# Ten expert loads ahead instead of six, whole experts for two of the three matrices, and further rounds before the last two quads

## The reference, cut to what matters

```python
for l in range(2):
    mod = silu(c) @ mod_w[l] + mod_b[l]        # 1024 x 6144: shift, scale, gate, twice
    h = rms_norm(x, norm1_g[l]) * (1 + scale1) + shift1
    x = x + gate1 * attention(h)               # w_in 1024 x 3072 (+8), w_out 1024 x 1024
    h = rms_norm(x, norm2_g[l]) * (1 + scale2) + shift2
    # router: one of 4 groups, then 2 of its 8 experts for each token
    # every expert: w1, w3: 1024 x 512, w2: 512 x 1024
    y = sum over experts of (silu(h @ w1[e]) * (h @ w3[e]) * gate[:, e]) @ w2[e]
    x = x + gate2 * y
```

## Time and profile before

| | |
|---|---|
| runs | 1378.91, 1379.0, 1375.66 us; median 1378.91 |
| the profiled execution | 1371.47 us, span 1369.7 us |
| data moved | 489.78 MB, 358 GB/s over the span |
| TensorE | busy 72% of the span, mean granted clock 0.868 |
| VectorE, ScalarE, GpSimd | busy 19%, 16%, 2% |
| experts of layer 0 and 1 | about 222 to 695 us and 893 to 1364 us |

### The profile page before, as it was taken

How to read it: one execution, slowest core, us unless ns; L and a number is a source line. 1 busy time by engine, 2 the same in 40 slices (tenths; PEclk the granted TensorE clock), 3 DMA queues, 4 the chain that set the end, 5 groups by cost and what they waited for, 6 DMA issues and landing times.

```text
span 1369.7 us, 13973 instructions
## 1 busy us (share of the span) xinstructions
PE 989.0 (72%) x5668; PEld 443.5 (32%) x5668; DVE 262.8 (19%) x573; ACT 213.9 (16%) x431; POOL 30.4 (2%) x89
## 2 busy tenths in 40 slices
PE   4999898667565766766679999967476675757665
PEld 1445555222121222222146665532121231212121
DVE  0545534101000010100020366410000010000101
ACT  2223314001000000100010353410000010000000
POOL 3000000000000000000000022000000000000000
PEclk9999999788887888888789999999887888878787
DMA  9973716999999999999999336569999999999995
GB/s 355 392 224 123 307 62 278 423 422 422 423 421 422 422 423 422 421 422 423 422 405 376 136 117 253 235 277 422 423 422 423 422 422 422 422 422 422 422 422 216
DMA packets 90826, 489.78 MB, mean 358 GB/s; under 512 B 18208, under 2 KB 18336, under 8 KB 37544
## 3 DMA queue, kind: packets, MB, share of 16 engines
q1 hardware_dynamic: 87776, 487.95, 87.4%
q10 hardware_dynamic: 3016, 1.37, 0.4%
HBM read 488.25 MB, written 1.05 MB: 357 GB/s over the span
## 4 chain that ended last, share of the span: by engine, by line
DMA 53%; PE 39%; DVE 4%; issue 1%; ACT 1%; SPq 1%; DVEq 0%
DMA ring<-in_moe_w_dram 52%; PE bank L546 8%; PE bank L788 7%; PE bank L813 7%; PE bank L586 4%; PE bank L699 4%; PE bank L511 2%; DMA ring<-in_mod_w_dram 1%; PE bank L638 1%; SPq L335 1%; PE bank L540 1%; PE bank L654 1%; PE bank L749 1%; PE bank L823 1%; DVE tmp L1404 0%
## 5 line engine op out<-in xcount | busy, mean ns | idle before, releaser
L788 PE MATMUL bank<-ring,region 128*32 128x512 f32 x2048 | 303.9, 748 | 189.2 <-DMA ring<-in_moe_w_dram 187.5
L813 PE MATMUL bank<-ring,region 128*32 128x512 f32 x1024 | 168.5, 818 | 122.9 <-DMA ring<-in_moe_w_dram 122.9
L788 PEld LDWEIGHTS bank<-ring,region 128*32 128x32 f32 x2048 | 83.6, 133 | 396.1 <-issue 394.4
L813 PEld LDWEIGHTS bank<-ring,region 128*32 128x32 f32 x1024 | 46.0, 143 | 232.7 <-issue 232.7
L546 PE MATMUL bank<-ring,hT 128*128 128x512 f32 x256 | 115.4, 602 | 2.7 <-ACT hT L953 2.7
L1542 DVE TENSOR_TENSOR region<-region,bank 128x512 f32<-128x512 f32 x16 | 11.0, 688 | 497.6 <-PE bank L788 497.6
L953 ACT ACTIVATE region<-bank,shift,scale 128x128 f32<-128x128 f32 x64 | 24.1, 457 | 353.2 <-PE bank L772 353.2
L1549 DVE TENSOR_TENSOR region<-bank,region 128x512 f32<-128x512 f32 x32 | 20.6, 686 | 281.1 <-PE bank L813 281.1
L823 PE MATMUL bank<-region 128*128 128x512 f32 x128 | 59.2, 605 | 13.4 <-DVE region L1549 13.4
L546 PEld LDWEIGHTS bank<-ring,hT 128*128 128x128 f32 x256 | 47.9, 193 | 59.4 <-issue 56.7
L511 PE MATMUL bank<-ring,c_wide 128*32 128x512 f32 x384 | 52.0, 670 | 18.0 <-DMA ring<-in_mod_w_dram 18.0
(11 more groups left out here) (217 smaller groups left out, 649.7 us busy)
## 6 DMA issues: line engine op xcount, KB each, us to landing
ring<-in_moe_w_dram SPq DMA_DIRECT2D x192, 2048.0 KB, 20.9
ring<-in_mod_w_dram SPq DMA_DIRECT2D x24, 2048.0 KB, 12.3
ring<-in_ev_w_in_dram SPq DMA_DIRECT2D x6, 2048.0 KB, 22.0
ring<-in_od_w_in_dram SPq DMA_DIRECT2D x6, 2048.0 KB, 19.2
ring<-in_ev_w_out_dram SPq DMA_DIRECT2D x2, 2048.0 KB, 7.6
ring<-in_od_w_out_dram SPq DMA_DIRECT2D x2, 2048.0 KB, 8.1
x<-in_x_dram ACTq DMA_DIRECT2D x1, 1024.0 KB, 5.1
out_dram<-x SPq DMA_DIRECT2D x4, 256.0 KB, 2.5
```

The lines of the kernel that those rows point to most:

```text
L788: last = pe.matmul(bank[which][32 * j:32 * j + 32, :], m.seated[:, 4 * part + k, 32 * j:32 * j + 32], w, start=(part == 0 and k == 0), sto ...
L813: last = pe.matmul(bank[half][32 * j:32 * j + 32, :], m.hidT[:, 2 * part + c, 32 * j:32 * j + 32], w, start=(part == 0 and c == 0), stop=( ...
```

## The change

It has four parts.

1. **Four more places.** `work` (over `gate1`, `raw`, `normed`, `tmp`, `tmp2`) and `tokens` (over `x` and `hT`) become slots 6 and 7 of a ring of eight, for expert units alone. `alone` is a place of its own, and `apart` is two halves, one over `att` (`sc`, `pr`, `pT`), one at the end of `region`. The last two hold units 10 and 11 of the last quad. `alone` is loaded after SECOND 3, the first half of `apart` after expert unit 2, the second after unit 7.
2. **Whole experts.** A unit of w1 or w3 is now one expert: one row of 16 KB in each partition. TensorE waits for all four units of w1 (or w3), makes 32 products, and the four slots are released together by its last four. Units of w2 stay as they are.
3. **Pairs of quads.** The loop runs three times over two quads; the last two quads are written out. In the last quad the parts of w2 are swapped: 10 and 11 first, then 8 and 9. SP issues 22 loads for the last two quads.
4. **Further rounds** stand before the last two quads on all engines.

```diff
+EXPERT_SLOTS = RING + 2
+PAIR_UNITS = 24
+ALONE = (10, 11)
+ALONE_AT = 15
+APART_AT = (2, 7)
...
-    m.x = sb("x", [P, TT, D])
+    m.alone = sb("alone", [P, KC * COL])
+    m.tokens = sb("tokens", [P, TT * D + KC * T])
+    m.work = sb("work", [P, 8 * COL])
+    m.att = sb("att", [P, 6 * ATT])
+    m.slots = [m.ring[:, i, :] for i in range(RING)] + [m.work[:, :], m.tokens[:, :]]
...
 def expert_unit(m, a, l, quad, u):
...
-    v = v[bass.ds(quad, 1), :, 2 * pair:2 * pair + 2, part * 2 * D:(part + 1) * 2 * D]
+    if which < 2:
+        v = v[:, :, rest:rest + 1, :]
+    else:
+        part, pair = divmod(rest, 2)
+        v = v[:, :, 2 * pair:2 * pair + 2, part * 2 * D:(part + 1) * 2 * D]
...
         for u in range(DENSE_UNITS):
-            g = g0 + u
-            if g >= RING:
-                sp.wait_ge(m.ring_used, g - RING + 1)
+            if l and u < RING:
+                sp.wait_ge(m.ring_used, g0 - EXPERT_SLOTS + 1 + (u if u < 4 else u + 2))
+            elif u >= RING:
+                sp.wait_ge(m.ring_used, g0 + u - RING + 1)
...
+            if u == ALONE_AT:
+                sp.dma_start(unit_tile(m.alone[:, :], ALONE[0]), expert_unit(m, a, l, QUADS - 1, ALONE[0])).then_inc(
+                    m.alone_full, 16)
...
-        with sp.Fori(0, QUADS) as quad:
-            for u in range(QUAD_UNITS):
-                g = g0 + u
-                sp.wait_ge(m.ring_used, g - RING + 1 + QUAD_UNITS * quad)
...
+        for i in range(PAIR_UNITS):
+            if i < RING:
+                sp.wait_ge(m.ring_used, g0 - RING + i + 1)
+            elif i == RING:
+                sp.wait_ge(m.s["x_added"], TT * (2 * l + 1))
+            elif i == RING + 1:
+                sp.wait_ge(m.s["h_chunked"], TT * (l + 1))
+                sp.wait_ge(m.s["x_placed"], l + 1)
+            else:
+                sp.wait_ge(m.ring_used, g0 + i - EXPERT_SLOTS + 1)
+            expert_load(i, i // QUAD_UNITS)
+            if i == APART_AT[0]:
+                sp.wait_ge(m.s["pv_done"], 12 + 16 * l)
+                apart_load(0)
+            if i == APART_AT[1]:
+                sp.wait_ge(m.s["row_made"], 4 * (l + 1))
+                apart_load(1)
+        with sp.Fori(1, LAST_PAIR) as d:
...
+        for i in range(PAIR_UNITS - len(ALONE)):
+            sp.wait_ge(m.ring_used, g0 + PAIR_UNITS * LAST_PAIR + i - EXPERT_SLOTS + 1)
+            expert_load(i, 2 * LAST_PAIR + i // QUAD_UNITS)
...
         for which in range(2):
-            for part in range(2):
-                u = 4 * which + 2 * part
...
+            for j in range(4):
+                landed(4 * which + j)
+            for k in range(KC):
...
+                for j in range(4):
+                    last = pe.matmul(bank[which][32 * j:32 * j + 32, :], m.seated[:, k, 32 * j:32 * j + 32],
+                                     tile(4 * which + j, 0)[:, k * FE:(k + 1) * FE],
...
+                    if k == KC - 1:
+                        last.then_inc(used, 1)
...
+        with pe.Fori(0, LAST_PAIR) as d:
+            two_quads(d, False)
+        further_rounds(l)
+        two_quads(LAST_PAIR, True)
```

More of the change, by code:

```diff
@@ L99, with plan_slots, expert_slot, expert_fill @@
 EXP_AND_LN = "natural_log_exp_and_others"
+def plan_slots():
+    filled = [0] * EXPERT_SLOTS
+    order = list(range(RING))
+    dense, expert = [], []
+    for l in range(DEPTH):
+        units = []
+        for u in range(DENSE_UNITS):
+            slot = order[u % RING]
+            filled[slot] += 1
+            units.append((slot, filled[slot]))
+        dense.append(units)
+        turn = DENSE_UNITS % RING
+        order = order[turn:] + order[:turn]
+        cycle = order + [RING, RING + 1]
+        expert.append((cycle, [filled[slot] for slot in cycle]))
+        for i in range(EXPERT_UNITS - len(ALONE)):
+            filled[cycle[i % EXPERT_SLOTS]] += 1
+    return dense, expert
+DENSE_AT, EXPERT_AT = plan_slots()
+SPARE = T
+def expert_slot(l, i):
+    return EXPERT_AT[l][0][i % EXPERT_SLOTS]
+def expert_fill(l, i):
+    return 16 * (EXPERT_AT[l][1][i % EXPERT_SLOTS] + i // EXPERT_SLOTS + 1)
+PAIR_FILLS = 16 * PAIR_UNITS // EXPERT_SLOTS
 class Chain:
@@ L764, in route, with quad_of_experts @@
                   skip_group_check=True).then_inc(s["ranked"], 1)
-    def quad_of_experts(e, n, seats_made, slots, landed, used):
+    def quad_of_experts(e, n, seats_made, tile, landed, used, parts=(0, 1)):
         pe.wait_ge(e["sel_made"], seats_made)
@@ L778, in quad_of_experts @@
         for which in range(2):
-            for part in range(2):
-                u = 4 * which + 2 * part
[L781 to L793, removed]
+            for j in range(4):
+                landed(4 * which + j)
+            for k in range(KC):
+                if which == 0 and k % 4 == 0:
+                    pe.wait_ge(e["seated_act" if k else "seated_dve"], 4 * n + 4)
+                for j in range(4):
+                    last = pe.matmul(bank[which][32 * j:32 * j + 32, :], m.seated[:, k, 32 * j:32 * j + 32],
+                                     tile(4 * which + j, 0)[:, k * FE:(k + 1) * FE],
+                                     start=(k == 0), stop=(k == KC - 1),
+                                     skip_group_check=True, tile_position=(0, 32 * j))
+                    if k == KC - 1:
+                        last.then_inc(used, 1)
         pe.wait_ge(e["gate_made"], n + 1)
@@ L802, in quad_of_experts @@
         pe.wait_ge(e["turned_copied"], 2 * n + 2)
-        for part in range(2):
+        for part in parts:
             u = 8 + 2 * part
@@ L1142, in experts @@
                     quad_of_experts(l, "more", (r - 1) * QUADS + quad)
+        with act.Fori(2 * LAST_PAIR, QUADS) as quad:
+            quad_of_experts(l, "first", quad)
     first_loads(act, m, a)
```

162 lines of the change are left out of this document (98 added, 64 removed).

## The result

The changed kernel takes 1331.34 us in the median of four runs (1330.91 to 1337.26), against 1377.59 us of before: ratio 0.9686, 95% interval 0.9662 to 0.971. Measured again beside the experiments it was 0.9702 (0.9675 to 0.9729). The profiled execution took 1331.2 us, 40.3 less than that of before; the prediction's sum had said 38.9 less. In microseconds the two medians of 1331.3 and 1333.2 stand at the lower edge of the predicted range (1333 to 1353), the first just outside; the two ratios, times the 1378.9 us that the forecast was scaled from, give 1335.6 and 1337.8.

A forecast was written before the change was run, and what follows sets the result against it. Expert stages were taken as bound by weight transfers, dense parts by TensorE. Terms -32.8 - 7.5 + 1.4 + 0 = -38.9 took the profiled 1371.5 to 1332.6 us, scaled to a median of 1340; range 1333 to 1353.

The forecast's parts named there:

- Part 1, -32.8 us: Expert stages: four more units loaded ahead at 4.98 us each, less 3.5, save 16.4 us per layer.
- The later first release: First quad: release after 64 records instead of 32, so the first refilled unit starts 3.5 us later per layer.
- The rival that the loads ahead come late: First quad: new waits in SP's queue put 1.5 units per layer back, +15 us, 1355; chance 0.10.
- Rows, -7.5 us: Long expert stretches: 16 KB rows at 428 GB/s take 1.35% less time for 112 units.
- The rival that longer rows give little: Long expert stretches: the rate stays at 422 GB/s, total 1347.3 us, or some 1344 by the skill; chance 0.24.
- Releases in fours, no hole: Ring of eight: slots come free before units are due, 3 us left at worst, so cost is nothing.
- The last quad, +2.3: After the last landing: w3 takes 8.8 us, then both w2 parts; end at T + 8.2 instead of T + 5.95.
- the rival of the cold seam: Last quad: w3 runs wholly at the lower clock, both seams cost 4.8 us more, about 1349; chance 0.06.
- Further rounds, -0.9: End of the program: moving the branch before a quad where TensorE waits anyway gives 0.9 us.
- the seam, 0: Between the layers: no change, with ends of -0.7 and +4.8 us.
- two paths through the seam: Between layers, from last landing T: TensorE reaches L846 at T + 13.1; loads land FIRST 3 at T + 21.8.

The follow-up runs named there:

- e4: The changed kernel with unit 6, and behind it unit 7 and unit 11's second half, also waiting for the first release: 1356.4 us, ratio 0.9861.
- e8: The changed kernel with w3 instead of w2 in the two extra places, and w2 in whole experts except in each layer's last quad: 1324.5 us, ratio 0.9641.
- e5: The kernel before, ring of six kept, with whole experts for w1 and w3 alone: 1437.2 us, ratio 1.0457.
- e2: The changed kernel, ring of eight kept, with 8 KB rows again and w1 and w3 in parts of two units released in twos: 1331.1 us, ratio 0.9696.
- e7: The changed kernel with the branch over the further rounds after the last quad again, on all engines: 1339.4 us, ratio 0.9746.
- e9: The changed kernel with units 0 to 3 of each layer's first quad in half rows of two experts, released in twos: 1331.9 us, ratio 0.9683.

## Why the prediction was right

*Part 1, -32.8 us.* Right, and shown: e4 gives 5.0 us for a unit. From the first w1 record to the last landing the changed kernel takes 18.9 and 20.4 us less than before in its first profile, 20.4 and 20.7 in its second; the sum had 16.4 + 3.75 = 20.2 per layer, rows included. The later first release, charged with 3.5 us per layer, measured 4.7 and 2.7, then 3.7 and 2.5. The rival that the loads ahead come late has fallen: unit 7 was issued 13 us before the first release.

*Rows, -7.5 us.* Right, and a little small: 8.4 by the time between landings, since a unit of long rows takes 1.5% less and not 1.35%; 428 GB/s by e8. The rival that longer rows give little has fallen. By the rule of the Trainium skill (DMA: Bandwidth & Descriptors, "Why small descriptors are slow") the gain would have been an estimated 3.2 us; the traces don't agree, they show more than twice that.

*Releases in fours, no hole.* Right for the long stretch, share 1.01; e5 shows how near the edge is. But the text gave whole experts a gain of 7.5 and put what they cost elsewhere: 7.0 for the first releases under part 1, 2.3 for w3 in one piece under part 3. Added up by what causes them, these terms are 1.8 us on the wrong side, and the experiment without part 2 (e2) shows 1.0, which is no difference on the ruler. The sum was right; that part 2 is worth nothing stood in it unread.

*The last quad, +2.3.* Off by little: w3 took 9.5 to 10.0 us instead of 8.8, the tail grew by 2.0 with the branch gone (+1.4 expected). At 13.6 us for w3 the rival of the cold seam would have stood; it has fallen.

*Further rounds, -0.9, and the seam, 0.* Both came out, at 1.0 (e7) and at 0.1 to 0.6 (29.1 us before, 29.2 and 29.7 after), the second in part by cancelling. The forecast had two paths through the seam. That of the loads ends last: FIRST 3 lands 22.7 and 23.1 us behind the last expert unit, 21.8 forecast. On TensorE's path the branch had been taken at its 3.7 us, without the 2.3 us of the lower clock behind it. With the branch elsewhere and w3 in two parts the seam is 26.4 us (e2); w3 in one piece and the later loads of FIRST bring it back to 29.7.

*The median.* 1340 was forecast, 1331 and 1333 measured. The forecast in the clock of the profiled execution was 1332.6, against 1331.2. It was scaled up by the median of the first three runs of before, 1378.9; by the 1375.5 of eleven later runs the same scaling gives 1336.4. So 3 us of the error are the scatter of before, and what is left is of the size by which repeats differ. It is not explained further.

## What to carry to other kernels

Where transfers bound a stage and idle in the stage ahead, count units: each one loaded ahead was worth its own transfer time here, and an idle tile of any other stage is a place for one. Before a unit is made coarser, write down when each slot is due and when it comes free, for the steady state, for the first release after the loads ahead and for the last landing; the two ends cost here what the longer rows gave. Then add the terms up by the part of the change that causes each, and not only by the place where it shows. A pause of a few us on the path costs more than itself if TensorE's work behind it starts at the lower clock.

## What the runs showed of the hardware

- A load of 2 MB in rows of 16 KB takes 4.894 us and one in rows of 8 KB 4.969, queued back to back, in the median; the profiles with such rows agree on both to 0.003 us. With the rows of 2 and 4 KB the rates are 387, 411, 422 and 428 GB/s, which lie on a straight line of time against length with about 9 ns at its foot. The two short sizes rest on one stretch of 15 and 12 us each, of other weights, and were not varied by experiment.
- TensorE's clock: behind a pause of 3.7 us the granted clock was 0.50, and 45 records of 128 x 32 by 512 took 7.8 us, without the pause 5.5.
- The start of the program and the dense part of layer 1 vary by 6.6 and 3.4 us from one execution to the next, with the expert stages steady to within 2 us. What makes the difference there was not looked into.
- Single loads of the long stretch land 0.3 to 1.6 us late (more than 5.25 us behind the one before): none in the kernel before, two in each profile of the changed kernel, seven in e9. The cause is open.
